# Attention weights kept in float32 once instead of split twice, in the first two attentions of a three-block transformer kernel

## What is computed

```
# layer 0 (nsa): 16 query heads of 64, 4 key/value heads, 4 query heads share one
o_cmp = softmax(q @ kcc.T / 8 + mask) @ vcc          # 31 compressed tokens
o_sel = attention over selected blocks (ks, vs)      # here all 8 blocks are selected, so causal over 512
o_win = banded_attention(q, kw, vw, window 512)      # also causal over 512
o = g0 * o_cmp + g1 * o_sel + g2 * o_win             # gates per head and row
# layer 1 (swa): 16 query heads, 2 key/value heads, window 128, a sink logit in the softmax
o = banded_attention(q, k, v, 128, sinks)
```

## Time and profile before

| | |
|---|---|
| time, median of 3 runs | 2871.19 us |
| the runs | 2868.43 to 2871.31 us |
| span of the profiled execution (its own time is not listed apart) | 2869.8 us |
| PE busy | 2622.8 us (91%), 11822 instructions |
| DVE busy | 1416.0 us (49%), 2716 instructions |
| ACT busy | 754.1 us (26%) |
| POOL busy | 1752.8 us (61%) |
| first attention (first to last instruction of its pipeline) | about 289 to 541 us |
| second attention | about 1076 to 1173 us |

### The profile page before, as it was taken

How to read it: one execution, slowest core, us unless ns; L and a number is a source line. 1 busy time by engine, 2 the same in 40 slices (tenths; PEclk the granted TensorE clock), 3 DMA queues, 4 the chain that set the end, 5 groups by cost and what they waited for, 6 DMA issues and landing times. The chain is left out here.

```text
span 2869.8 us, 36833 instructions
## 1 busy us (share of the span) xinstructions
PE 2622.8 (91%) x11822; PEld 2087.3 (73%) x11822; DVE 1416.0 (49%) x2716; ACT 754.1 (26%) x1559; POOL 1752.8 (61%) x971
## 2 busy tenths in 40 slices
PE   5899788889999897889999899997999899999998
PEld 3687666668888676768888687775787777787876
DVE  5557777544433368441112366766116734563452
ACT  3300666431111217340011322322104613200001
POOL 2645333457777565557777544442677876787784
PEclk9899788999999997999999999998999999999999
DMA  6465000126545230223333222211243232233332
GB/s 219 142 197 158 1 1 1 37 89 211 168 145 167 70 74 1 93 72 95 95 95 95 90 65 59 59 54 36 73 105 74 57 87 95 83 95 102 88 106 70
DMA packets 420399, 260.08 MB, mean 91 GB/s; under 512 B 62828, under 2 KB 411369, under 8 KB 413745
## 3 DMA queue, kind: packets, MB, share of 16 engines
q1 hardware_dynamic: 390368, 193.18, 23.4%
q10 hardware_dynamic: 29905, 65.31, 6.7%
HBM read 254.25 MB, written 8.10 MB: 91 GB/s over the span
## 5 line engine op out<-in xcount | busy, mean ns | idle before, releaser
L613 POOL TENSOR_TENSOR W<-RAW,zeros 128x1024 fp32r<-128x1024 f32 (+2 forms) x355 | 679.8, 1915 | 827.7 <-PE PA L684 428.5
L620 POOL TENSOR_TENSOR W<-RAW,W 128x1024 fp32r<-128x1024 f32 (+2 forms) x355 | 853.6, 2404 | 29.4 <-PE PA L688 3.0
L683 PE MATMUL PA<-H,W 128*128 128x512 f32 x1312 | 524.1, 399 | 12.2 <-DVEq L1531 6.6
L684 PE MATMUL PA<-H,W 128*128 128x512 f32 x1312 | 513.5, 391 | 0.0
L683 PE MATMUL PA<-A,W 128*128 128x512 f32 x944 | 381.2, 404 | 16.2 <-DVE A L1736 11.4
L684 PE MATMUL PA<-A,W 128*128 128x512 f32 x944 | 378.2, 401 | 0.0
L688 PE MATMUL PA<-H,W 128*128 128x512 f32 x1312 | 324.2, 389 | 0.0
L683 PEld LDWEIGHTS PA<-H,W 128*128 128x128 f32 x1312 | 247.8, 189 | 73.0 <-issue 11.9
L684 PEld LDWEIGHTS PA<-H,W 128*128 128x128 f32 x1312 | 248.0, 189 | 55.7 <-issue 4.6
L688 PEld LDWEIGHTS PA<-H,W 128*128 128x128 f32 x1312 | 246.3, 188 | 51.1
L688 PE MATMUL PA<-A,W 128*128 128x512 f32 x944 | 241.6, 398 | 0.0
(11 more groups left out here) (345 smaller groups left out, 4056.6 us busy)
## 6 DMA issues: line engine op xcount, KB each, us to landing
AD<-in_ada_w_dram ACTq DMA_DIRECT2D x40, 1024.0 KB, 5.5
RAW<-in_w_in_dram SPq DMA_DIRECT2D x160, 256.0 KB, 3.2
RAW<-in_mlp_w_up_dram SPq DMA_DIRECT2D x128, 256.0 KB, 3.1
RAW<-in_mlp_w_down_dram SPq DMA_DIRECT2D x128, 256.0 KB, 3.0
RAW<-in_w_up_dram SPq DMA_DIRECT2D x88, 256.0 KB, 3.1
RAW<-in_nsa_w_in_dram SPq DMA_DIRECT2D x40, 256.0 KB, 3.9
RAW<-in_w_down_dram SPq DMA_DIRECT2D x16, 384.0 KB, 3.6
RAW<-in_swa_w_in_dram SPq DMA_DIRECT2D x20, 256.0 KB, 3.4
```

The costliest lines, as they stand in the source:

```text
L613: e.tensor_tensor(W[0][:, s, 0:kc], RAW[:, s, 0:kc], zeros[:, 0:1].rearrange("p (a b) -> p a b", b=1).broadcast_to([P, kc, P]), ALU.add).t ...
L620: e.tensor_tensor(W[1][:, s, 0:kc], RAW[:, s, 0:kc], W[0][:, s, 0:kc].bitcast(F32), ALU.subtract).then_inc(w_split, 1)
L683: pe.matmul(PA[s][:, 0:n], W[0][:, s, k], hi, start=(k == 0), stop=False)
L684: mm = pe.matmul(PA[s][:, 0:n], W[0][:, s, k], lo, start=False, stop=False)
```

## The change

In the first two attentions (`plan.whole` is true) the turned weights leave their bank once, as float32, into KEPT (three quarters of the units by ACT, the last unit of each group, `by_dve`, by DVE; the compressed unit's by ACT into CKEPT). The value product takes them and the unsplit values (VS, VW, VCC, as float32): one float32 product in place of two float32r ones for each slice of keys. The 128 columns of values are two key/value heads side by side, of which 64 output rows count; DVE copies these into OT (`"kept"`), and ACT's copy of half of PO and the add are gone. The values' splits are gone. Every step of age is one less: the copy at step j+6 on either engine, the value product at `last + 7`. The keys have four pairs of buffers (KK0, KK1 for even key/value heads, KK2, KK3 for odd ones), and the splits for key/value heads 1 to 3 are issued by ACT at the first (KS) and fifth (KW) step of the last query head that uses the old keys. The new buffers lie over H, the low tmps and freed space. The other attentions keep the old way.

```diff
-            self.weights, self.turn, self.hi, self.lo, self.av = (pr, 5, 6, 7, 11) if in_h else (pr[:4], 3, 3, 4, 8)
+            self.weights, self.turn, self.hi, self.lo, self.av = (pr, 5, 6, 6, 10) if in_h else (pr[:4], 3, 3, 4, 8)
...
+            self.by_dve = [self.whole and b == 3 for _, b in self.units]
...
                 if j == 0:
-                    last = 9 * (h - 1) + 4 * n + 3
-                    plan.split(("k", n, g), last + 1 if g else 2 * n, last if g else None, split_k(KK[n], K[lo:lo + HD, g // 2, :], lo))
-                    plan.split(("v", n, g), last + plan.out - 3 if g else 2 * n + 1, G - 3 + n if g else None, split_v(VV[n], V[:, :, g * HD:g * HD + HD]))
+                    plan.split(("k", n, g), 9 * (h - 1) + 4 * n if g else 2 * n, 9 * (h - 5) + 4 * n + 3 if g >= 2 else None,
+                               split_k(KK[n + g % 2 * 2], K[lo:lo + HD, g // 2, :], lo))
...
-                    values=[(VV[n][:, t, :], x, t, t, NT) for t in range(NT) for x in range(2)],
-                    store=(plan.turned, n * NT), prev=G + n - 3,
+                    values=[(V[:, t, g // 2 * P:g // 2 * P + P], 0, t, t, NT) for t in range(NT)],
+                    store=([KEPT[h % 2]], n * NT), prev=G + n - 6,
...
-                values=[(VC2[:, g, :], x, 0, 0, NT) for x in range(2)],
+                values=[(VCC[:, g // 2 * 2:g // 2 * 2 + 2, :].rearrange("p a d -> p (a d)"), 0, 0, 0, NT)],
...
-                values=[(VV[g][:, t, :], x, t, a, z) for t in range(NT)
-                        for x, a, z in ([(0, t, t + 1), (0, t + 1, t + 2)] if 0 < t < NT - 1 else [(0, t, min(t + 2, NT))]) + [(1, t, min(t + 2, NT))]],
+                values=[(VS[:, t, 0:P], 0, t, a, z) for t in range(NT)
+                        for a, z in ([(t, t + 1), (t + 1, t + 2)] if 0 < t < NT - 1 else [(t, min(t + 2, NT))])],
...
-                        pe.wait_ge(sem("pt_lo"), u - len(banks) + 1)
+                        kept(j - len(banks))
...
-                    pe.wait_ge(sem("pt_lo"), u0 + last + 1)
+                    kept(last)
...
-                    act.activation(turned_part(plan, j, 0), turned_bank(plan, j), ACT.Copy).then_inc(sem("pt_hi"), 1)
+                    if not plan.by_dve[j]:
+                        act.wait_ge(sem("pt_turned"), u + 1)
+                        if b % (4 // plan.halves) == 0 and grp["prev"] >= 0:
+                            act.wait_ge(sem("attended"), g0 + grp["prev"] * plan.halves + b * plan.halves // 4 + 1)
+                        act.activation(turned_part(plan, j, 0), turned_bank(plan, j), ACT.Copy).then_inc(sem("kept_act" if plan.whole else "pt_hi"), 1)
...
-                    dve.tensor_tensor(turned_part(plan, j, 1), turned_bank(plan, j), turned_part(plan, j, 0).bitcast(F32),
-                                      ALU.subtract).then_inc(sem("pt_lo"), 1)
+                    if plan.by_dve[j]:
+                        prev = plan.groups[plan.units[j][0]]["prev"]
+                        dve.wait_ge(sem("pt_turned"), u0 + j + 1)
+                        if prev >= 0:
+                            dve.wait_ge(sem("attended"), g0 + prev + 1)
+                        dve.tensor_copy(turned_part(plan, j, 0), turned_bank(plan, j)).then_inc(sem("kept_dve"), 1)
...
+                    elif out and out[0] == "kept":
+                        hd, lo = c["halves"], out[2]
+                        dve.wait_ge(sem("attended"), g0 + (G + 1) * plan.halves)
+                        dve.tensor_copy(out[1], PO[hd % 2][lo:lo + HD, :]).then_inc(sem("head_out"), 1)
```

More of the change, by code:

```diff
@@ L12 @@
+import itertools
 from contextlib import ExitStack
@@ L121, in build @@
         ADAH = sb("ADAH", [P, 4, ADA_N], F32, over)
+    with ExitStack() as over:
+        KEPT = [sb(f"KEPT{i}", [P, DC, S], F32, over) for i in range(2)]
     H = [sb(f"H{i}", [P, DC, S], F32R) for i in range(2)]
@@ L135, in build @@
         TURN0 = sb("TURN0", [P, 4, S], F32R, over)
+    with ExitStack() as over:
+        CKEPT = sb("CKEPT", [P, 2, S], F32, over)
+        KK3 = [sb(f"KK3{x}", [P, S], F32R, over) for x in "hl"]
     tmp += [sb(f"tmp{i}", [P, S]) for i in range(2, 6)]
@@ L182, in build @@
         KK = [[sb(f"KK{i}{x}", [P, S], F32R, over) for x in "hl"] for i in range(2)]
+        with ExitStack() as one:
+            KK += [[sb(f"KK2{x}", [P, S], F32R, one) for x in "hl"], KK3]
         VV = [sb(f"VV{i}", [P, NT, P], F32R, over) for i in range(2)]
@@ L407, in build @@
     HIDDEN = [hid, tmp[5][:, 0:8 * NCMP].rearrange("p (a n) -> p a n", a=2)]
-    TURNED = {True: [H[x][:] for x in range(2)],
-              False: [TURN0[:], TURN1[:]]}
+    TURNED = [TURN0[:], TURN1[:]]
     def qcols(b):
@@ L450, in number @@
                 self.units += [(G, 0)] if grp["all"] else [(G, b) for b in range(4)]
+            self.by_dve = [self.whole and b == 3 for _, b in self.units]
+            self.kept_act = list(itertools.accumulate(int(self.whole and not d) for d in self.by_dve))
+            self.kept_dve = list(itertools.accumulate(int(d) for d in self.by_dve))
             self.read, self.done = {}, {}
@@ L489, in plan_nsa @@
                 plan.groups.append(dict(
-                    need=[("q", h), ("k", n, g)], need_v=("v", n, g), head=h, first=n == 0, out=None, rows=P, keys=[(b + 1) * P for b in range(NT)],
-                    at=[0] * NT, scores=[stacked_scores(h, KK[n], b, 0, (b + 1) * P) for b in range(NT)],
-                    values=[(VV[n][:, t, :], x, t, t, NT) for t in range(NT) for x in range(2)],
-                    store=(plan.turned, n * NT), prev=G + n - 3,
+                    need=[("q", h), ("k", n, g)], need_v=None, head=h, first=n == 0, out=None, rows=P, keys=[(b + 1) * P for b in range(NT)],
@@ L497, in plan_nsa @@
             plan.groups.append(dict(
-                need=[("q", h)], need_v=("v", 2, 0), head=h, first=False, out=("halves", OF[(h % 2) * HD:(h % 2) * HD + HD, h // 2, :]), rows=NCMP,
+                need=[("q", h)], need_v=None, head=h, first=False, rows=NCMP,
+                out=("kept", OF[(h % 2) * HD:(h % 2) * HD + HD, h // 2, :], lo),
                 keys=[NT * NCMP], at=[0], scores=[[(q[:, qcols(b)], KCC[lo:lo + HD, g // 2, :]) for b in range(NT)]],
-                values=[(VC2[:, g, :], x, 0, 0, NT) for x in range(2)],
@@ L922, in attention @@
             c["splits"] += len(plan.at)
+            if plan.whole:
+                c["kept_act"] += plan.kept_act[-1]
+                c["kept_dve"] += plan.kept_dve[-1]
+            else:
+                c["pt_lo"] += n
         def mlp(ada=False):
```

40 lines of the change are left out of this document (27 added, 13 removed).

## The result

| | before | after |
|---|---|---|
| median (4 runs each, same chip) | 2871.25 us (2868.43 to 2873.61) | 2888.51 us (2886.87 to 2892.19) |
| span of the profiled execution | 2869.8 us | 2887.5 us |
| first output of a head to the last, first attention | 320.85 to 540.86 | 321.87 to 569.55 |
| the same, second attention | 1097.56 to 1172.04 | 1124.49 to 1187.12 |
| from there to the end | 1697.8 us | 1700.4 us |

The ratio is 1.0061, 95% interval 1.0047 to 1.0074: slower by 0.6%, where -7 us was forecast. The table adds up to the spans' difference of +17.7 us. The first attention's outputs take 247.68 us instead of 220.01, and they start 1.0 later: +28.7. The second attention, with what lies ahead of it, gets 13.6 shorter, and the rest 2.6 longer, which no run takes apart. So two large terms of opposite sign moved, and the first attention is where the forecast fell.

A forecast was written before the change was run, and what follows sets the result against it. First attention was read as a chain of coupled engines, none full; second as DVE nearly full. First attention's heads -0.9, its start and end +1, second attention -6.8 and -0.5 sum to -7.2: 2864.0 us, range 2843 to 2886.

The forecast's parts named there:

- The step that failed: First attention: PE waits of about 1.0 us for DVE's copy, twice a head, were taken to leave the clock full.
- The walk: Step-by-step sum of the first attention's new head at full clock: 6.5 us KS to KW, 8.9 us back.
- The head at full clock: First attention: a clean head takes 15.3 us, 2 us more than before.
- Value products on PE: A first-attention group's product grows from 1.33 to 2.35 us; the second attention's product takes 1.9 us.
- Change of keys: First attention: the splits' stall goes to nothing; 13 heads take 198.9 us against 199.84, -0.9 us.
- Start and tail: First attention's start and last two heads: together +1 us, bounds -1 and +4.
- Second attention: Heads of 5.0 us, twelve in 60.0 against 66.76, -6.8 us; PE 94% full, clock stays up.
- The clock still falls: Rival, chance 0.14: in the first attention three half-clock episodes of 18 us stay, +23 us, giving 2887.
- a fuller TensorE would be safer: Argument against the falling clock: throttling is the default and activity releases it, so a fuller PE keeps its clock.
- PE is the only bound: Rival, chance 0.18: DVE and ACT keep up, first-attention heads cost PE's own 13.5 to 14.2 us; 2844 us.
- The head is longer: Rival, chance 0.18: ACT's copy ends last, or second (+10) or first attention (+12) heads run longer; 2871 to 2876.
- the stall remains: Rival, chance 0.08: ACT's splits still delay an exponential at key changes and the clock falls; +20 us, 2884.

The follow-up runs named there:

- experiment 6: Three kernels: old first attention with new second, 2858.30 us; that plus double-buffered keys, 2862.53 us; changed kernel with single-buffered keys, 2889.09 us.
- experiment 1: Changed kernel with the two transposes ahead of each first-attention KS value product made four times instead of once; 2864.14 us, 0.9971 of before.
- the refilled kernels: Changed kernel with the transposes ahead of each first-attention KS value product made four times (2864.14 us) or twice (2862.29 us) instead of once.

## Why the prediction was wrong, point by point

**The step that failed** is the sentence "The clean head shows waits of this kind at 1.00 clock throughout, so I take the clock as full." The waits of the old head were 0.50, 0.39 and 0.50 us ahead of value products. The walk itself put the new one at about 1.0 us, twice as long, and called it the same kind. Its rows held no value product with a wait between 0.50 us (clock kept) and 1.92 us (clock fell), so the clock at 1.0 us was unknown and should have been bounded from both sides. The trace of before has waits in between, ahead of value products at full clock: 0.80 us (423.41) and 0.98 us (538.04), and one of 1.79 us (403.49) behind which the clock had fallen. They would have bounded it, but not shown the fall, since a wait as long as the new one had kept the clock there. At 1.66 us a fall, once in each head, it is +22 us over thirteen heads, and turns -7 into slower.

**The head at full clock** was right: 15.3 us walked, 15.48 measured where the wait is covered. From after itself, 17.07-1.66 = 15.41. Its parts too: the KS to KW stretch has the copy at its end, and the late copy behind three small sums is where the walk put it.

**Value products on PE.** 2.35 us forecast for a group, 2.15 measured at full clock, from 0.86 us for 512 columns. A product that is 2.5 times 512 columns long thus takes 0.86 us for 512, as the earlier trace rows say, and only the 0.2 added for its end was not there. The prediction cited a sustained spacing of about 131 ns from the Trainium skill, TensorE: Matmul & The Clock Gate, section Back-to-back issue gap, by which the group would be an estimated 1.3 us; no value product here was that short. The same section of the Trainium skill has a figure for single products, N/2.4 + 2.5 ns, 215.8 ns at 512 columns. It comes to an estimated 2.16 us for the prediction's four passes over 1280 columns, and with that the trace agrees. (The prediction's "the group would gain only some 0.3" does not follow from its 0.52 us: 2.5 times 0.52, with the 0.2 for the end, against 1.33 is a gain of about 0.2. Nothing else used it.)

**Change of keys.** The forecast of no stall came true in after, but its reason, buffers that nobody reads, is only a small part. In experiment 6 the stall is still there with them alone (1.92 us), and the changed kernel without them waits 0.7 to 0.85 us longer once at each change, where the old one waited 1.5 us longer at two products. What else left those steps in the new scheme is the splits of the values and the low halves; no run took these alone, so that cause is argued, not shown.

**Start and tail.** +1 for both together, with a bound of +4, was forecast; +1.0 at the start and +5.6 at the tail came, so the bound was too low. Part of the tail is the clock again: the clock there is 0.87, and in experiment 1 the stretch from the fourteenth output to the last is 22.43 us instead of 25.74, against 20.17 before.

**Second attention.** The direction, the mechanism and the clock (1.00) were right, the size was small: twelve heads 60.0 forecast, 54.12 measured. The mis-sized term is first the product, 1.54 us instead of 1.9: 896 columns at 0.86 us for 512 are 1.51, so its records, ten of twelve with 128 columns only, cost what their columns say, and even the lower bound of 1.7 was too high. With the remaining steps 0.1 to 0.2 shorter, the head is 4.5 and not 5.0. TensorE is 87% busy there (47.01 of 54.12), not 94%. This gave 6 us that hid a part of the loss.

**The rivals.** "The clock still falls" gave 2887, and 2888.5 came, but the number is luck: it was priced as three long episodes, each about a change of keys, and decided "once PE's idle time comes near the 1.92 us". What happened is fifteen short ones, one in each head from the second on, at half that idle time. Its argument against itself, that a fuller TensorE would be safer, drew on the Trainium skill, TensorE: Matmul & The Clock Gate, section What's actually happening; in this case TensorE was busy for 188.23 of 221.94 us, 85% against 82% in the earlier trace rows, and its clock fell in each of these thirteen heads. A mean busy share did not tell where the clock falls. The Trainium skill, TensorE: Matmul & The Clock Gate, section HAM oscillation — how this bites in real kernels, describes a wait that throttles TensorE anew in every tile of a loop, so that each tile pays for it. Its waits are 3 to 5 us long. The trace of after shows the same pattern, once in each of fifteen heads, at a wait of 0.99 us, far below that example's; the measurement decides. "PE is the only bound" needed one more step of age and is then real: 13.74 us a head against its 14.0, 2839 against its 2844. "The head is longer" did not occur, nor did "the stall remains".

## What to carry to other kernels

When a change makes an engine wait a little longer at the same place in every round, the clock has to be bounded there, not carried over: at a wait of 0.99 us the clock fell and cost 1.66 us in each of fifteen heads, and two needless transposes gave it back. That the same wait elsewhere kept the clock is no proof: in these traces equal waits at the same place had both outcomes. When an operation gets longer on the engine that stands in order (here the value product, 1.3 to 2.2 us), the work ahead of it needs as much distance as before or more; the change took a step of distance away, and giving it back is worth 50 us. Undo each part of a change alone before crediting it: here the second attention and DVE's copy carried it, and the doubled buffers changed the whole by nothing that could be measured. And read the trace where two totals agree: there the buffers saved 2.4 us of waiting, which two heads at another clock made up for.

## What the runs showed of the hardware

- At the place ahead of the KS product the granted clock stayed at 1.00 behind waits of 0.31, 0.34 and 0.77 us. Behind 0.86 us (ACT copying the last block) it fell in seven heads of ten, behind 0.99 and 1.00 us in every such head of after but not in all with single-buffered keys. At the KW product 1.13 and 1.47 us never lowered it, and 0.61 us (the product in two) once did. In two heads of the refilled kernels it fell while TensorE shows as busy. So the length of the wait ahead does not settle it; what else does is open.
- A fall behind such a short wait lasted some 3.4 us and ended while TensorE multiplied; those of before at the changes of keys lasted longer. The windows of the kernel before in which the clock was 0.50 throughout:

```profile
410.00:420.00 10.00, 8.55 (x34) 7.29 (x34) 7.40 (x24) 4.70 (x14) 2.68 (x4) 0.50 0.00 0
470.00:480.00 10.00, 8.42 (x31) 6.80 (x31) 7.04 (x24) 6.82 (x18) 2.96 (x5) 0.50 0.00 0
```

- Float32 products cost by their columns down to records of 128: 1280 columns in eight records took 2.15 us, 896 columns in twelve records 1.54 us, 0.86 and 0.88 us for each 512.
